# Two of four weight sums per group moved from VectorE to GpSimd in a three-block transformer kernel

## The reference

```python
def swiglu(x, w_gate, w_up, w_down):
    return (jax.nn.silu(x @ w_gate) * (x @ w_up)) @ w_down
...
    for i in range(DEPTH):                       # DEPTH = 2
        h = rmsnorm(x, g_ffn1_pre[i])
        x = x + 0.5 * rmsnorm(swiglu(h, w1_gate[i], w1_up[i], w1_down[i]), g_ffn1_post[i])
...
        h = rmsnorm(x, g_ffn2_pre[i])
        x = x + 0.5 * rmsnorm(swiglu(h, w2_gate[i], w2_up[i], w2_down[i]), g_ffn2_post[i])
```

## Time and profile before

| | us |
|---|---|
| median of 3 runs (lowest, highest) | 2809.68 (2808.68, 2810.14) |
| time of the profiled execution | 2810.25 |
| its span, first to last instruction | 2808.1 |
| TensorE busy | 2782.1 (99%) |
| VectorE busy | 1850.4 (66%) |
| ScalarE busy | 1364.3 (49%) |
| GpSimd busy | 36.6 (1%) |

### The profile page before, as it was taken

How to read it: one execution, slowest core, us unless ns; L and a number is a source line. 1 busy time by engine, 2 the same in 40 slices (tenths; PEclk the granted TensorE clock), 3 DMA queues, 4 the chain that set the end, 5 groups by cost and what they waited for, 6 DMA issues and landing times.

```text
span 2808.1 us, 40633 instructions
## 1 busy us (share of the span) xinstructions
PE 2782.1 (99%) x16458; PEld 2430.5 (87%) x16458; DVE 1850.4 (66%) x2548; ACT 1364.3 (49%) x2120; POOL 36.6 (1%) x38
## 2 busy tenths in 40 slices
PE   9999999999999999999999999999999999999999
PEld 7998887699998899988976789988987889888888
DVE  7884466768873588863567588843876746666437
ACT  6553343565552575552526555533755535323235
POOL 0000000000000000000000000000001100000000
PEclk9999999999999999999999999999999999999999
DMA  5332323033422234332241233323233222332331
GB/s 169 98 106 94 120 57 96 19 102 98 121 91 90 84 92 121 96 98 97 76 100 46 91 90 92 113 90 113 76 94 93 87 91 91 113 97 91 107 119 60
DMA packets 266217, 265.28 MB, mean 94 GB/s; under 512 B 34992, under 2 KB 218672, under 8 KB 266032
## 3 DMA queue, kind: packets, MB, share of 16 engines
q1 hardware_dynamic: 265888, 262.68, 31.0%
q10 hardware_dynamic: 144, 0.00, 0.0%
HBM read 258.44 MB, written 2.10 MB: 93 GB/s over the span
## 4 chain that ended last, share of the span: by engine, by line
PE 95%; DVE 3%; ACT 2%; issue 1%; DMA 0%; SPq 0%; DVEq 0%; ACTq 0%
PE banks L667 30%; PE banks L669 29%; PE banks L668 29%; PE banks L1171 1%; PE banks L1193 1%; ACT HF L1555 1%; PE banks L1230 1%; PE banks L1182 1%; DVE SF L2249 0%; PE banks L1234 0%; DVE HL L2040 0%; ACT WH L541 0%; PE banks L1220 0%; PE banks L706 0%; PE banks L1324 0%
## 5 line engine op out<-in xcount | busy, mean ns | idle before, releaser
L667 PE MATMUL banks<-HH,WH 128*128 128x256 f32 (+1 forms) x2876 | 963.3, 335 | 15.3 <-DVE VE L2240 14.4
L668 PE MATMUL banks<-HH,WL 128*128 128x256 f32 (+1 forms) x2876 | 957.6, 333 | 0.0
L669 PE MATMUL banks<-HL,WH 128*128 128x256 f32 (+1 forms) x2876 | 957.1, 333 | 0.0
L546 DVE TENSOR_TENSOR WL<-raw,WH 128x1024 fp32r<-128x1024 f32 (+2 forms) x414 | 498.4, 1206 | 618.9 <-ACT WH L541 618.2
L541 ACT ACTIVATE WH<-raw 128x1024 fp32r<-128x1024 f32 (+2 forms) x414 | 429.3, 1040 | 693.7 <-PE banks L669 469.3
L667 PEld LDWEIGHTS banks<-HH,WH 128*128 128x128 f32 x2876 | 548.5, 191 | 76.9 <-issue 23.1
L668 PEld LDWEIGHTS banks<-HH,WL 128*128 128x128 f32 x2876 | 548.7, 191 | 52.4 <-issue 1.0
L669 PEld LDWEIGHTS banks<-HL,WH 128*128 128x128 f32 x2876 | 548.5, 191 | 52.2
L667 PE MATMUL banks<-HIDH_HIGH,WH 128*128 128x512 f32 (+1 forms) x832 | 298.5, 359 | 3.1 <-DVE HIDF L2283 1.7
L668 PE MATMUL banks<-HIDH_HIGH,WL 128*128 128x512 f32 (+1 forms) x832 | 296.9, 357 | 0.0
L669 PE MATMUL banks<-HIDL_LOW,WH 128*128 128x512 f32 (+1 forms) x832 | 296.9, 357 | 0.0
(11 more groups left out here) (317 smaller groups left out, 3322.1 us busy)
## 6 DMA issues: line engine op xcount, KB each, us to landing
raw<-in_w_down SPq DMA_DIRECT2D x112, 512.0 KB, 3.3
raw<-in_w_up SPq DMA_DIRECT2D x172, 256.0 KB, 3.1
raw<-in_w_in SPq DMA_DIRECT2D x68, 512.0 KB, 3.7
raw<-in_w_gate SPq DMA_DIRECT2D x76, 256.0 KB, 3.3
extra_raw<-in_w_gate SPq DMA_DIRECT2D x68, 256.0 KB, 3.9
extra_raw<-in_w_up SPq DMA_DIRECT2D x68, 256.0 KB, 4.8
raw<-in_w_ple_gate SPq DMA_DIRECT2D x24, 512.0 KB, 3.4
raw<-in_w_out SPq DMA_DIRECT2D x16, 512.0 KB, 3.8
```

Source lines behind the costliest of these rows:

```text
L546: e.tensor_tensor(WL[tile_of[u]][:, 0:n], raw[raw_of(u)][:, 0:n], WH[tile_of[u]][:, 0:n].bitcast(F32), ALU.subtract).then_inc(*low.done((u,)))
L667: e.matmul(o, wh, ah, start=start, stop=False, skip_group_check=skip)
L668: e.matmul(o, wl, ah, start=False, stop=False, skip_group_check=skip)
L669: return e.matmul(o, wh, al, start=False, stop=stop, skip_group_check=skip)
```

## The change

Sums 4 and 6 of each group of seven products are computed by GpSimd instead of VectorE; sums 1 and 2 stay. GpSimd gets a loop over the groups of each of the four stages. For sum 4 it waits until quarter (1, 1) has landed and VectorE has made sum 1, the last reader of (0, 1). For sum 6 it waits until (1, 0) has landed and the low split of product 2, the last reader of the earlier sum in (0, 0), is done. The splits of products 4 and 6, and the tile that is given back after sum 6, wait on GpSimd's count instead of VectorE's.

```diff
             if q == (1, 0):
-                return vec.at("weight_sum", s, g, 6)
+                return pool.at("weight_sum", s, g, 6)
...
-                e.wait_ge(*(quarter_landed(s, g, SPLIT_OF[ph]) if ph in (0, 3, 5) else vec.at("weight_sum", s, g, ph)))
+                e.wait_ge(*(quarter_landed(s, g, SPLIT_OF[ph]) if ph in (0, 3, 5) else
+                              (vec if ph < 3 else pool).at("weight_sum", s, g, ph)))
...
-            into, other = {1: ((0, 0), (0, 1)), 2: ((0, 0), (1, 1)), 4: ((0, 1), (1, 1)), 6: ((0, 0), (1, 0))}[ph]
+            into, other = {1: ((0, 0), (0, 1)), 2: ((0, 0), (1, 1))}[ph]
...
             for g in SEVEN_GROUPS:
-                vector_weight_sum(e, s, g, 4)
...
                 split_low(e, W[s, "seven", g, 5])
-                vector_weight_sum(e, s, g, 6)
                 split_low(e, W[s, "seven", g, 6])
...
+        def gpsimd_weight_sums(e, s):
+
+            for g in SEVEN_GROUPS:
+                for ph, into, other, free in ((4, (0, 1), (1, 1), vec.at("weight_sum", s, g, 1)),
+                                              (6, (0, 0), (1, 0), low.at(W[s, "seven", g, 2]))):
+                    e.wait_ge(*quarter_landed(s, g, other))
+                    e.wait_ge(*free)
+                    target = raw_quarter(s, g, into)
+                    e.tensor_tensor(target[:], target[:], raw_quarter(s, g, other)[:], ALU.add).then_inc(*pool.done(
+                        ("weight_sum", s, g, ph)))
+
         def gpsimd_program(e):
             for s, kind in enumerate(STAGES):
+                if s in SEVEN:
+                    gpsimd_weight_sums(e, s)
```

## The result

| | before | after |
|---|---|---|
| median, us (lowest to highest) | 2809.18 (2808.65 to 2810.14) | 2865.38 (2863.31 to 2865.87) |
| profiled execution, its span | 2810.25, 2808.1 | 2863.31, 2861.2 |

The ratio is 1.0198, with a 95% interval of 1.0181 to 1.0216: the change costs 56.2 us, 2.0%. The forecast was 2861 us in a range of 2826 to 2876.

The account below looks back on a forecast made before the run. TensorE, busy 99% of the span, was taken as the bound. Waits of 1.83 us in 7 groups of 4 stages, 28 in all, add 51.2 us to 2810.25 (2809.68 median): 2861 us forecast, range 2826 to 2876.

Parts of the forecast that it names:

- the tight place: Product 2 of a group: TensorE needs p1, behind the silu and half scale 1; predicted wait 1.83 us, 28 times.
- P: Duration of one GpSimd sum of 1024 elements: taken as 2.35 us, lower bound 1.89, upper bound 2.43.
- 2P - 2.87: Formula for TensorE's wait ahead of product 2 in each paying group, from both collisions: 1.83 us.
- spare time: From p1's end to product 2, less 0.15 us to start: half scale 1 may come 0.43 us later without a wait.
- Sum 4's collision: GpSimd's sum 4 holds VectorE's low split of product 1, making it and the queue behind 1.23 us late.
- Sum 6's collision: GpSimd's sum 6 runs after half hidden 0 and holds half scale 1: 2.26 us late, 1.13 gain included.
- a hold to the very end: If VectorE were held until GpSimd's end, without the last 0.14 us off, the sum would be 8 us larger.
- What costs nothing: Low split 3, product 4, transfers and GpSimd's own queue with its mix stage were predicted to add no TensorE wait.
- A: Rival: only sum 6 collides on the path; wait 0.60 us, 28 times, 2827 us; chance 0.06.
- B: Rival: VectorE keeps the turn when its next instruction is queued, so half scale 1 is 0.10 late; 2810 us; chance 0.05.
- C: Rival: no mutual hold between VectorE and GpSimd for these instructions; TensorE stays busy, 2810 us; chance 0.06.
- D: Rival: each of the 28 waits also costs half clock speed for 3 us, 42 us more, 2903 us; chance 0.05.

Follow-up runs that it names:

- Experiment 4: The changed kernel with the copy p1 ahead of the silu of half 1 in ScalarE's order: 2809.99 us, ratio 1.0001.
- experiment 1: Against the kernel before, only sum 4 moved to GpSimd, sum 6 back on VectorE: 2810.03 us, ratio 1.0002.
- experiment 2: Against the kernel before, only sum 6 moved to GpSimd, sum 4 back on VectorE: 2860.59 us, ratio 1.0183.
- experiment 3: The changed kernel, both sums on GpSimd, with sum 6 also waiting for half scale 1: 2809.05 us, ratio 0.9998.
- experiment 5: The changed kernel with sum 6 over 512 of its 1024 columns, the other half left out: 2834.67 us, ratio 1.0092.
- experiment 6: The changed kernel with sums 4 and 6 each replaced by three GpSimd fills of the same tile: 2809.86 us, ratio 1.0002.

## Why the prediction was right

**The bound and the tight place.** As forecast, the loss is one wait ahead of product 2 in groups 3 to 9, 28 in all, each for p1 behind the silu behind half scale 1. Experiment 4 shows the chain: with p1 out of it the loss is gone.

**The duration of a sum.** The term that was a little small: I took P = 2.35 from two shapes, and the sum takes 2.40 to 2.41. The formula 2P - 2.87 gives 1.95 with 2.41, which is the growth of the period just measured; 1.83 was forecast. The missing 0.12 us a group, 3 us in all, is most of the distance from 2861 to 2865. That it fits to the hundredth is in part luck: sum 1 starts 0.05 us later behind product 2 of the group before than I had it (8.31 us for 8.26), and the spare time is larger by as much. The lower bound of 1.89, from an addition that isn't in place, was far off.

**Sum 4's collision.** 1.23 us late forecast, 1.29 measured (2.51 for 1.22), with 1.28 from the formula at P = 2.40.

**Sum 6's collision.** Released at the end of low split 2, GpSimd waited out half hidden 0 (to 100.58) and ended at 102.83, 2.25 behind it: P - 0.15, where the earlier trace rows had given P - 0.14. Half scale 1 was held for 2.21 us and went on as from 102.70, 0.13 before GpSimd's end. The tail of 0.14 us from the earlier trace rows is there again, so the 8 us that a hold to the very end would have added didn't come. The removed sum 4 gave back its 1.13 us, as experiments 1 and 2 show from both sides.

**Spare time.** 0.43 us was right to a tenth: p1 to product 2 took 0.10 after, where I had 0.15.

**What costs nothing.** Low split 3, product 4, transfers and GpSimd's mix work stayed out of TensorE's waits.

**Rivals.** Experiments 3 to 6 settle the cause together: the loss goes with the order alone (3, 4), with the length of GpSimd's sum (5) and with its reading (6). A fell with the stretched low split of product 1, B with the 28 stretched half scales. C, no hold, fell with the stretched rows, and experiment 6 shows what it would have looked like. D, the clock: over 56 to 220 the granted clock stayed at 1.00 with seven waits in it.

```profile
56.00:220.00 164.00, 151.90 (x1255) 150.69 (x1254) 134.83 (x118) 81.94 (x107) 35.89 (x14) 1.00 0.33 92
```

**One sign misjudged.** I had said that the waits would name p1; they named the split that ended 0.02 us before it. By my own list that would have counted as wrong.

## What to carry to other kernels

Work taken off an engine that nobody waits for is worth nothing, and moved to GpSimd it can hold the very engine it was to relieve: look where the moved instruction will run, which VectorE instructions with two SBUF inputs stand there, and how much spare time the chain behind them has. Here the loss of 56 us was a matter of order alone, and one more wait on GpSimd or one copy moved on ScalarE takes it away. The 18 us that could be won lay in the wait that stood first in TensorE's list, and one step too far in the same place lost them again.

## What the runs showed of the hardware

- GpSimd, once it waits, got its turn between two VectorE instructions standing back to back, and held the second until 0.13 to 0.14 us before its own end. In the kernel after this holds for all 28 groups: the 64 half scales take 106.0 us where they took 44.1, which is 28 holds of 2.21 us.
- An addition in place of 128x1024 float32 takes GpSimd 2.40 us, where VectorE takes 1.22. A fill of the same size takes 0.95 us and holds nobody (experiment 6).
- In stage 0 of the kernel after, waits of TensorE of some 1.7 us, once every 22 us, left the granted clock at 1.00. The four waits for the variance in the kernel before were followed by different clocks: 2.84 us by 0.50 (36 to 39), 4.28 us by 0.50 (635 to 638), 2.98 us by 1.00 (1050 to 1053) and 4.27 us by 0.63 (1647 to 1650). In the kernel after, the first of them, 2.57 us there, was followed by 0.60. What tells them apart stays open.
